# Delta rule: both directions' triangles in one matrix, and each engine's step ordered by a table of 13 rounds

## The reference, cut to what matters

```python
def bidir(q, k, v, g, beta, s_f, s_b):
    o_f, s_f = gated_delta_chunked(q, k, v, g[:, :, 0], beta[:, :, 0], s_f)
    fl = lambda a: jnp.flip(a, axis=1)
    o_b, s_b = gated_delta_chunked(fl(q), fl(k), fl(v), fl(g[:, :, 1]), fl(beta[:, :, 1]), s_b)
    return o_f + fl(o_b), s_f, s_b
```

## Time and profile before

| | us |
|---|---|
| median of 3 runs | 4530.08 (4506.61 to 4532.8) |
| the profiled execution, its own time | 4527.1 |
| its span (first to last instruction) | 4525.2 |
| PE, DVE, ACT, POOL busy | 3787.4, 2847.2, 1274.9, 1212.4 |
| granted TensorE clock, mean (share of full speed) | 0.942 |
| the stage of this change in the trace, 1238 to 2100 | 862 |

### The profile page before, as it was taken

The page is one execution under the profiler, slowest core; times in us unless marked ns, Lnnn a source line. Parts: engine busy times, 40 slices in busy tenths (PEclk is TensorE's granted clock), DMA queues, the critical chain, the costliest instruction groups (busy, mean ns, idle before and its releaser), DMA issues.

```text
span 4525.2 us, 42849 instructions
## 1 busy us (share of the span) xinstructions
PE 3787.4 (84%) x13298; PEld 2111.1 (47%) x13298; DVE 2847.2 (63%) x5758; ACT 1274.9 (28%) x3337; POOL 1212.4 (27%) x1220
## 2 busy tenths in 40 slices
PE   7879879998878898887898987787779777877777
PEld 3334447643467677766754542232223245422222
DVE  3756547767666676764487747767755545777544
ACT  1231110025311222212133333343333321333333
POOL 0001100001033333431033333343344400344333
PEclk9889989999988898989999999999999998999999
DMA  5423235544200000003399999999999932899998
GB/s 212 177 102 127 97 130 191 218 158 170 84 11 24 5 24 6 26 6 151 149 363 389 374 371 421 421 400 421 421 409 413 422 133 84 343 418 421 411 421 365
DMA packets 140147, 1073.78 MB, mean 237 GB/s; under 512 B 15504, under 2 KB 15888, under 8 KB 21520
## 3 DMA queue, kind: packets, MB, share of 16 engines
q0 software_dynamic: 112608, 820.04, 44.3%
q1 hardware_dynamic: 27312, 251.02, 14.6%
HBM read 1060.51 MB, written 10.49 MB: 237 GB/s over the span
## 4 chain that ended last, share of the span: by engine, by line
PE 42%; DVE 21%; DMA 18%; issue 11%; POOL 6%; ACT 3%; DVEq 0%; POOLq 0%; SPq 0%; ACTq 0%
PE bank L199 20%; DMA arena<-in_uv,arena 16%; POOL arena L2956 5%; PE bank L2924 5%; DVE arena L2973 4%; PE bank L2423 3%; ACT arena L211 2%; PE bank L2146 2%; DVE arena L443 2%; PE bank L2138 2%; DVE arena L217 2%; PE bank L1620 2%; DVE arena L561 2%; DVE arena L221 2%; PE bank L2125 1%
## 5 line engine op out<-in xcount | busy, mean ns | idle before, releaser
L2924 PE MATMUL bank<-arena 128*128 128x512 f32 x3072 | 1492.0, 618 | 360.9 <-ACT arena L211 359.1
L211 ACT ACTIVATE arena<-arena 128x1 f32<-128x1 f32 (+5 forms) x2631 | 867.4, 330 | 2020.3 <-DVE arena L2973 1138.0
L199 PE MATMUL bank<-arena 128*128 128x256 f32 (+4 forms) x4640 | 1304.5, 440 | 86.0 <-ACT arena L211 38.1
L2973 DVE CUSTOM_DVE_ANT_0 arena<-arena 128x1024 f32<-128x1024 f32 x768 | 941.3, 1226 | 636.8 <-DMA arena<-in_uv,arena 608.4
L2924 PEld LDWEIGHTS bank<-arena 128*128 128x128 f32 x3072 | 542.5, 191 | 1283.2 <-ACT arena L211 844.0
L2956 POOL DMA_INDIRECT arena<-in_uv,arena x768 | 786.6, 1024 | 1294.3 <-PE bank L2924 889.0
L199 PEld LDWEIGHTS bank<-arena 128*128 128x128 f32 (+2 forms) x4640 | 807.6, 196 | 569.6 <-issue 425.2
L211 ACT ACTIVATE arena<-bank 128x512 f32<-128x512 f32 (+3 forms) x448 | 245.6, 548 | 1092.2 <-PE bank L2125 498.1
L2208 POOL TENSOR_TENSOR arena<-arena 128x512 f32<-128x512 f32 x128 | 163.6, 1278 | 452.4 <-PE bank L2138 445.6
L443 DVE CUSTOM_DVE_ANT_0 arena<-arena 128x1024 f32<-128x1024 f32 x192 | 241.1, 1256 | 32.4 <-DMA arena<-in_w_rows 20.6
L2146 PE MATMUL bank<-arena 128*128 128x128 f32 x1024 | 156.2, 302 | 86.0 <-DVE arena L2167 86.0
(11 more groups left out here) (250 smaller groups left out, 2780.2 us busy)
## 6 DMA issues: line engine op xcount, KB each, us to landing
arena<-in_w_rows SPq DMA_DIRECT2D x50, 1024.0 KB, 4.8
arena<-in_w_in SPq DMA_DIRECT2D x16, 2048.0 KB, 8.4
arena<-in_wq SPq DMA_DIRECT2D x14, 2048.0 KB, 8.5
arena<-in_dn_w SPq DMA_DIRECT2D x12, 2048.0 KB, 9.1
arena<-in_w_up SPq DMA_DIRECT2D x11, 2048.0 KB, 8.4
arena<-in_dn_wo SPq DMA_DIRECT2D x8, 2048.0 KB, 10.9
arena<-in_w_rows POOLq DMA_DIRECT2D x14, 1024.0 KB, 6.1
arena<-in_uv,arena POOLq DMA_INDIRECT x768, 12.8
```

The costliest lines, as they stand in the source:

```text
L199: t = p.e.matmul(out, l, r, start=(i == 0), stop=(i == n - 1))
L211: return a().activation(out, in_, f, **kw)
L2924: t = p.e.matmul(by[half], m["dg"][ee % 4], m["uv"][r][:, 1024 + 512 * half:1536 + 512 * half], start=(ee == 0), stop=(ee == 127))
L2973: v().tensor_tensor_reduce(self.spare, uv[:, 0:1024], m["ht"][n % 2], 1.0, 0.0, ALU.mult, ALU.add, m["acts"][:, ee:ee + 1]).then_inc(*V.up ...
```

## The change

Both directions' triangles share one matrix per chunk: E holds the minimum of the two decays (one direction's difference is negative in the lower triangle, the other's in the upper), key products are made once per chunk, and the inverse runs on one matrix W. Per level DVE now does three operations from a bank (R masked transpose, T scaled by beta, W minus x) and POOL two masks (off-diagonal N, triangle B). At the end POOL cuts W into the two directions' triangles. Beta enters by small tables (`dve_beta`, `pe_beta`, `act_beta`) made once. Decay rows are stored to device memory and read back broadcast by SP DMAs (`sp_decay`, `sp_queries`) in place of broadcast products. Block k is prepared in slot k-1, inverted in slot k, staged (`*_stage`: queries, triangles, beta v) in slot k+1 and run through the recurrence in slot k+2. Each part is a table of 13 rounds, and in the recurrence the directions alternate: PE part 0 to 3 of direction d is in round 2 part + d. There are 18 slots instead of 17, and the projection's eight products are in rounds 0, 6, 8 and 9 to 12.

The diff, cut to its core; removed lines are those of the functions printed above and are left out. The recurrence's ScalarE copies are in rounds 3 and 4, its sums of squares in 6 to 10.

```diff
+        for d in range(2):
+            s.wait_ge(*self.V.of("ng.gx", d))
+            s.e.dma_start(self.crest[d], self.L["dn"]["gcr"][d]).then_inc(*self.D.up("crest.out", d))
...
+    def sp_decay(self, s, m, k):
+        ab = "ab"[k % 2]
+        if k > 1:
+            s.wait_ge(*self.V.of("pr.min", k - 2))
+        if k > 3:
+            for d in range(2):
+                s.wait_ge(*self.G.of("pr.tri", self.pair_of(d, k - 4), d))
+        for d in range(2):
+            dst = m["F"][k % 2] if d else m["E"][k % 4]
+            s.e.dma_start(heads(dst, 4), self.decay_rows(d, k, k % 4)).then_inc(*self.D.up(f"pg{d}{ab}.in", k))
+    def sp_queries(self, s, m, k):
+        if k % 4 == 0:
+            return
+        for d in range(2):
+            if k > 1:
+                s.wait_ge(*self.P.of("re.o", k - 2, d))
+            s.e.dma_start(heads(m["Q"][d][k % 2], 4), self.decay_rows(d, k, self.chunk_of(d, k))
+                          ).then_inc(*self.D.up(f"pq{d}{'ab'[k % 2]}.in", k))
...
+    def dve_beta(self, v, m):
+        V = self.V
+        v.wait_ge(*self.D.of("masks.in", 0))
+        for d in range(2):
+            be = m["BE"][:, d].rearrange("p t h -> p (t h)")
+            v().tensor_tensor(heads(m["W"][d], 64), bc(be, 2, 8), bc(m["start"][:, 4 * d, :], 1, 64), ALU.mult
+                              ).then_inc(*V.up("bt.z", d))
+        for l in range(4):
+            bs = m["BS"][:, l]
+            ts(v, bs, m["BE"][:, 0], m["side"][:, 0, l:l + 1], None, ALU.mult, None).then_inc(*V.up("bt.s0"))
+            v().scalar_tensor_tensor(bs, m["BE"][:, 1], m["side"][:, 1, l:l + 1], bs, ALU.mult, ALU.add
+                                     ).then_inc(*V.up("bt.s", l))
...
...
+        for r in range(self.ROUNDS):
+            if r == 0:
+                for d in range(2):
+                    self.dve_decay(v, m, k, d)
+            if r == 1:
+                E = m["E"][k % 4]
+                v().tensor_tensor(E, E, m["F"][k % 2], ALU.min).then_inc(*self.V.up("pr.min", k))
+            if r == 3:
+                E = m["E"][k % 4]
+                v.wait_ge(*self.A.of("pr.e", k))
+                ts(v, E, E, TINY, TINY, ALU.add, ALU.subtract).then_inc(*self.V.up("pr.cut", k))
+            if r in (4, 5):
+                self.dve_products(v, m, k, r - 4)
+            if r == 6:
+                self.dve_block(v, m, k, 0)
+                self.dve_block(v, m, k, 1)
+            if r == 7:
+                self.dve_block(v, m, k, 2)
+            if r > 8:
+                self.dve_substitute(v, m, k, r - 9)
             yield
     def dve_decay(self, v, m, k, d):
+    def dve_block(self, v, m, k, part):
+        V, (g, c), raw = self.V, divmod(k, 4), m["t8"][:, 0:4]
+        if part == 0:
+            v.wait_ge(*self.G.of("in.prod", k))
+            red(v, raw, m["prod"].rearrange("p (h b r) -> p h r b", h=4, b=16), ALU.add).then_inc(*V.up("in.raw"))
         if part == 1:
+            v.wait_ge(*self.A.of("bt.r", 1))
+            for d in range(2):
+                v().tensor_tensor(m["AC"][:, d], raw[:, :, ::-1] if d else raw, m["BR"][:, d, c, 4 * g:4 * g + 4, :], ALU.mult
+                                  ).then_inc(*V.up("in.AC"))
         if part == 2:
+    def dve_substitute(self, v, m, k, part):
...
...
...
+        P, V, G, W = self.P, self.V, self.G, m["W"][k % 2]
+        for r in range(self.ROUNDS):
+            n, part = divmod(r, 3)
+            l = n + 3
+            if part == 0 and l < 7:
...
+                    t = p.e.transpose(b[:, H4[h]], W[:, H4[h]], self.ident)
+                t.then_inc(*P.up("in.tr", k, l))
+                self.banks.give(("in.tr", k, l), V.of("in.R", k, l))
+            if part == 1:
+                p.wait_ge(*G.of("in.N", k, l))
+                p.wait_ge(*V.of("in.R", k, l))
+                b = self.banks.take(p, "in.y", k, l)
...
+                    t = p.e.matmul(b[:, H4[h]], m["N"][:, H4[h]], m["R"][:, H4[h]], start=True, stop=True)
+                t.then_inc(*P.up("in.y", k, l))
+                self.banks.give(("in.y", k, l), V.of("in.T", k, l))
+            if part == 2:
+                p.wait_ge(*V.of("in.T", k, l))
+                p.wait_ge(*G.of("in.B", k, l))
...
...
+        def off(k, l):
+            if k or l > 3:
+                g.wait_ge(*P.of("in.y", *((k, l - 1) if l > 3 else (k - 1, 6))))
+            g().tensor_tensor(heads(m["N"], 4), heads(m["AT"][k % 2], 4), bc(m["off"][:, l - 3, :], 1, 4), ALU.mult
+                              ).then_inc(*G.up("in.N", k, l))
+        def tri(l):
+            g.wait_ge(*V.of("in.W", k, l - 1))
+            if k or l > 3:
+                g.wait_ge(*P.of("in.x", *((k, l - 1) if l > 3 else (k - 1, 6))))
+            g().tensor_tensor(heads(m["B"], 4), heads(W, 4), bc(m["tri"][:, l - 3, :], 1, 4), ALU.mult
+                              ).then_inc(*G.up("in.B", k, l))
+        for r in range(self.ROUNDS):
+            if r == 0:
+                if k == 0:
+                    g.wait_ge(*V.of("pr.A", 0))
+                    off(0, 3)
+                tri(3)
+            if r in (2, 6, 8):
+                off(k, {2: 4, 6: 5, 8: 6}[r])
+            if r in (3, 7, 9):
+                tri({3: 4, 7: 5, 9: 6}[r])
+            if r == 11 and k < 15:
+                g.wait_ge(*V.of("pr.A", k + 1))
+                off(k + 1, 3)
+            if r == 12:
+                g.wait_ge(*V.of("in.W", k, 6))
+                for d, sg in ((1, -1), (0, 1)):
+                    if k > 1:
+                        g.wait_ge(*P.of("re.vn", k - 2, d))
+                    self.pool_triangle(g, self.inverse_at(m, d, k), W, sg).then_inc(*G.up("in.XT", k, d))
+            yield
+    def pool_triangle(self, g, out, x, sg):
+        return g().affine_select(out=heads(out, 4), in_=heads(x, 4), compare_op=ALU.is_ge, fill=0.0, base=0,
+                                 pattern=[[0, 4], [sg, 128]], channel_multiplier=-sg)
...
+    def act_stage(self, a, m, k):
+        for r in range(self.ROUNDS):
+    def pool_stage(self, g_, m, k):
+        P, V, A, G = self.P, self.V, self.A, self.G
+        g = k // 4
+        b22 = lambda x: x.rearrange("p (g h n) -> p g h n", g=2, h=2)
+        for r in range(self.ROUNDS):
             for d in range(2):
+                c = self.chunk_of(d, k)
+                if r == 1:
+                    pair = self.pair_of(d, k)
+                    g_.wait_ge(*V.of("pr.P", pair))
+                    if k > 1:
+                        g_.wait_ge(*P.of("re.o", k - 2, d))
+                    self.pool_triangle(g_, m["O"][d][k % 2], m["E"][pair % 4], -1 if d else 1).then_inc(*G.up("pr.tri", k, d))
+                if r == 4 and k % 4:
+                    Q = m["Q"][d][k % 2]
+                    g_.wait_ge(*A.of("pr.q", k, d))
+                    g_().tensor_tensor(b22(Q), b22(Q), bc(m["qT"][:, 2 * g:2 * g + 2, H4[c]], 2, 2), ALU.mult
+                                       ).then_inc(*G.up("pr.Q", k, d))
+                if r == 10:
+                    if k:
+                        g_.wait_ge(*(P.of("re.s", k - 1, d) if (k - 1) % 4 < 3 else P.of("re.vn", k - 1, d)))
+                    g_().tensor_tensor(heads(m["V2"][d], 4), heads(m["v"][:, c, 512 * g:512 * g + 512], 4),
+                                       bc(m["BE"][:, d, c, 4 * g:4 * g + 4], 2, 128), ALU.mult).then_inc(*G.up("re.bv", k, d))
+            yield
...
+        for r in range(self.ROUNDS):
+            if r in (1, 2) and st > 0:
+                carry(r - 1)
+            if r in (4, 5) and st < 3:
+                decay(r - 4)
+            if r in (5, 6):
+                output(r - 5)
+            if r in (7, 8) and st < 3:
+                state(r - 7)
+            if st == 3 and r in (3, 4, 11, 12):
+                norm({3: 0, 4: 1, 11: 2, 12: 3}[r])
+            yield
...
...
     def sp_zsteps(self, s, m):
+        s.wait_ge(*self.D.of("xrest.out", 0))
+        for d in range(2):
+            s.wait_ge(*self.D.of("crest.out", d))
+        for k in range(2):
+            self.sp_decay(s, m, k)
         for k in range(16):
             c, i = divmod(k, 4)
             if i == 0:
@@ -2449,19 +2471,37 @@
                     for _ in range(3):
                         self.ring.skip()
                 self.ring.load(s, self.I["dn_w"][8 + c], 8, 512)
+            if k < 14:
+                self.sp_decay(s, m, k + 2)
             s.wait_ge(*self.A.of("nz.z", k))
             s.e.dma_start(self.zrest[i][:, 512 * c:512 * c + 512], m["zst"][k % 2]
                           ).then_inc(*self.D.up(f"zout{'ab'[k % 2]}.out", k))
+            self.sp_queries(s, m, k)
+    def chunks(self, first, slot):
+        run(first)
+        for k in range(18):
...
+    def pe_chunks(self, p, m):
+        self.chunks(self.pe_prep(p, m, 0), lambda k: (
+            (self.pe_inverse(p, m, k), k < 16), (self.pe_prep(p, m, k + 1), k < 15), (self.pe_zstep(p, m, k), k < 16),
+            (self.pe_recur(p, m, k - 2), k > 1)))
+    def dve_chunks(self, v, m):
```

(54 more changed lines are left out.)

618 lines of the change are left out of this document (242 added, 376 removed).

## The result

The changed kernel takes 4343.9 us (median of four runs, 4339.5 to 4351.9) against 4531.4 for the kernel before on the same chip; the ratio on record is 0.9603, 95% interval 0.9578 to 0.9627 (the two medians alone would give 0.9586; one of the four runs of the kernel before took 4506.6 and the others 4530 to 4534). The profiled executions have spans of 4345.3 and 4525.2 us, 180 less. Forecast were 208 less.

A forecast was written before the change was run, and what follows sets the result against it. Before the change, TensorE, stretched by chains through VectorE and by its clock, bounds the stage. Terms -202 - 41 - 1 + 8 + 28 = -208 us take 4527.1 to 4319; 3.0 more gives 4322, range 4238 to 4405.

The forecast's parts named there:

- The bound: In the fourteen slots VectorE takes over from TensorE as the bound, busy 27.3 us a slot without contention.
- A slot: Each of the fourteen slots: 27.3 + 1.4 + 3.3 + 4 + 1 = 37.0 us; together 518, 202 less.
- The lock: VectorE operations with two SBUF inputs lengthen while POOL works beside them: 3.3 us more a slot.
- Gate weights: Before blocks 4, 8 and 12 a 2 MB load stalls TensorE: 9.3 us each, +28, bounds 0 and 36.
- First two slots: Slots without recurrence, set by the chain of inverse levels: 27 us each, 54 for 95, -41.
- tail: End of the stage: the recurrence lags two slots, so two blocks run alone; 30 us, +8.
- DMAs added: Four decay and query reads of 256 KB a block: 4 us each to land, hidden, sum unchanged.
- (d): Rival: query reads come late and ScalarE waits, 5 us in 12 slots, +60, 4382 us; chance 6%.
- (b): Rival: the slot keeps today's loss of 13.8 us and takes 42.5; +77, 4399 us; chance 13%.
- (a): Rival: lock, clock and POOL waits all hide, slot 31.5 us; 77 less, 4245 us; chance 15%.
- (c): Rival: TensorE's clock sags part of each slot, costing 8 us a slot; +112, 4434 us; chance 8%.
- (e): Rival: TensorE's lower share keeps it at 1.2 GHz throughout, slower than before; 4667 us; chance 3%.

The follow-up runs named there:

- the fastest version: Against the changed kernel: gate products in earlier rounds, substitution's product written back into its bank, output and state copies moved to ScalarE; 4268.7 us, ratio 0.9420.

## Why the prediction was right, and which terms were off

The forecast was 4322, the median is 4343.9: 22 above, inside the range and within the forecast case's own. The mechanism was right; the sizes of some terms were off.

- **The bound.** That VectorE takes it over was right, and is shown from both sides: work added on VectorE costs 0.99 of itself, work added on TensorE 0.08 and 0.22. VectorE is busy 81% in the full slots; in the stalled slots it is 64% and in the last, which prepares nothing, 59%. Over all fourteen it is 75%, so the sign of being wrong, under 70%, did not come.
- **A slot.** Forecast 37.0 for each of fourteen. The ten full, unstalled ones between 1322.25 and 1858.55 have 38.5, the last, which prepares no block, 29.4. VectorE's busy time is 31.2 (93.77/3) against 27.3 + 3.3 = 30.6, idle time 7.3 against 1.4 + 4 + 1 = 6.4. Thirteen at 38.5 and one at 29.4 are 529.9, 12 over the 518.
- **The lock.** By the sums of the rows (decays 7.5 above 0.69 each, min 3.6, block columns 14 and substitutions 31 above 0.19, cut and norm the rest) it is some 72 us in the stage, 4.5 a block, 2.2 more than the 2.3 of before; I took 3.3. The places were right: decays 924 ns, small substitutions up to 909, where the earlier trace rows had 361 on the mean. The term was 1.1 too high, and the counted operations, 31.2 - 2.2 = 29.0 a slot against 27.3, too low: the two hid each other.
- **Gate weights: the term most off for its size.** Forecast 9.3 a stall from the landing time, +28; measured 12.0 each by the slots (151.5 - 3 x 38.5 = 36), and 35 by the run that removes it. The wait for the DMA was near (10.1); missing was what follows it, TensorE at half clock after ten idle microseconds (2.07 us for the two passes at 1408.30). It stood in the text as the upper end, 36. That the stall goes away when the last use moves two rounds forward and the next first use three back, I did not see.
- **First two slots** 58.8 for 54, **preparation** 24.5 for 24 (cut at 1263.5, where the first gate product starts), **tail** 31.5 for 30. The clock of the first two slots was 0.89.
- **DMAs added.** The decay reads landed after 5.5 us and the query reads after 4.9 (medians) where I took 4; all but one were hidden in the fourteen slots. The 256 KB stores of the gate projection, in the same kernel, landed after 3.5.
- **Sum of the differences:** 12 + 8 + 5 + 0.5 + 1.5 = 27; the stage took 681, not 654. The profiled execution was 28 above its forecast and the median 22, because I added 3.0 from one to the other, where here the median is 3.2 below. TensorE's clock in full slots, 0.86 to 0.96, seems to have cost little, for TensorE has slack; the filler that raised it in the fastest version gained nothing.
- **The rivals.** In the fourteen slots ScalarE waited once for a DMA of this kind, 5.1 us (d). The mean full slot was 38.5, not 42.5 (b) or 31.5 (a). The 8 us a slot of a clock that sags (c) did not come, though the clock of the full slots was 0.86 to 0.96; TensorE at 1.2 GHz throughout (e) is excluded by the same figures. In the three slots with a stall the clock was 0.83, in the last slot 1.00. I had expected gaps of 1 to 2 us; three full slots began with 2.9 to 4.8, where VectorE's norms stand ahead of the block expansion. The Trainium skill's rule ("TensorE: Matmul & The Clock Gate", HAM oscillation) that idle gaps put the clock down fits the stalls; the shorter gaps of the full slots did so in part.

## What to carry to other kernels

After an edit that takes a third from one engine, count the next engine's operations with the prices of the trace and add the contention of operands in SBUF; here its work then set the time almost one to one, while the order of the hand-offs was worth 27 us. Before trusting that, look for a single-buffered load whose last use and first use have come to lie next to each other: moving the uses five rounds further apart gave 35 us, as much as any other edit here. Price a stall as the wait plus the half clock after it.

## What was not expected of the hardware

Columns added to TensorE raised its own clock: 110 us of gate products cost 9 us, and three full slots went from 0.93 to 1.00. The 110 us in the chain cost 24, with the full slots at 0.91 to 1.00. In the fastest version three more products a slot again raised the clock and changed the time by 2.5 us, within the interval. Products on 16 rows ran partly at half clock in two kernels (336 and 362 ns on the mean) and at full clock in a third (276): the row count was not the reason.

The contention with POOL moves when it is taken out in one place: 32 us less in the substitutions were 25 us less for VectorE as a whole, and copies taken from VectorE saved 7 us of contention beside their own 17.
